# Rotations and a spread of row maxima in a hybrid attention block: one product of plain numbers against two of rounded parts

## The reference

```python
def apply_axial_rope(x, cos, sin):
    xs = x.reshape(shp[0], shp[1], shp[2], 2, 2, ROPE_HALF)
    x1 = xs[..., 0, :]
    x2 = xs[..., 1, :]
    out = jnp.stack([x1 * cc - x2 * ss, x2 * cc + x1 * ss], axis=-2)
```

```python
def _partial_rope(u, pos):
    u1 = u[..., :half]
    u2 = u[..., half:ROPE_DIM]
    r1 = u1 * cos - u2 * sin
    r2 = u2 * cos + u1 * sin
```

```python
        m_t = jnp.maximum(inter, jnp.max(logD, axis=-1))
        w_inter = jnp.exp(inter - m_t)
        s = jnp.einsum('bhld,bhsd->bhls', qc, kc) * jnp.exp(logD - m_t[..., None])
```

## Time and profile before

| what | value |
|---|---|
| median of 3 runs | 1625.29 us (1624.4 to 1625.34) |
| the profiled execution | 1620.71 us |
| its span in the profile | 1619.0 us |
| PE busy | 1539.4 us, 95% |
| PEld busy | 1229.6 us, 76% |
| DVE, ACT, POOL busy | 747.5, 639.8, 685.0 us |
| mean granted clock of PE | 0.98 of full speed |

### The profile page before, as it was taken

The page is one execution under the profiler, slowest core; times in us unless marked ns, Lnnn a source line. Parts: engine busy times, 40 slices in busy tenths (PEclk is TensorE's granted clock), DMA queues, the critical chain, the costliest instruction groups (busy, mean ns, idle before and its releaser), DMA issues.

```text
span 1619.0 us, 25305 instructions
## 1 busy us (share of the span) xinstructions
PE 1539.4 (95%) x9954; PEld 1229.6 (76%) x9954; DVE 747.5 (46%) x1723; ACT 639.8 (40%) x1337; POOL 685.0 (42%) x660
## 2 busy tenths in 40 slices
PE   5999999999898999999998899999999989999997
PEld 3787777777587888787876687878787867766875
DVE  4434554554533434444355454733432564455253
ACT  4244444444532533333344353434332344443331
POOL 2534344443532533434334444535255434444462
PEclk9999999999999999999998899999999999999998
DMA  9111111110133222323231222222131221111221
GB/s 396 43 69 53 35 45 53 53 53 27 53 105 104 79 79 79 105 79 105 79 105 52 79 85 79 79 72 85 52 104 53 98 85 53 53 53 53 99 84 52
DMA packets 22149, 128.22 MB, mean 79 GB/s; under 512 B 2448, under 2 KB 2576, under 8 KB 8080
## 3 DMA queue, kind: packets, MB, share of 16 engines
q1 hardware_dynamic: 21888, 126.35, 22.0%
q10 hardware_dynamic: 144, 0.26, 0.1%
HBM read 124.50 MB, written 2.10 MB: 78 GB/s over the span
## 4 chain that ended last, share of the span: by engine, by line
PE 83%; DVE 8%; ACT 3%; issue 3%; POOL 2%; DMA 1%; SPq 0%; POOLq 0%; DVEq 0%; ACTq 0%
PE PS L1440 16%; PE PS L1442 15%; PE PS L1441 15%; PE PS L1520 7%; PE PS L1530 6%; PE PS L1555 6%; PE PS L1435 3%; PE PS L1436 3%; PE PS L1437 3%; DVE sm L2129 1%; PE PS L1608 1%; PE PS L1600 1%; PE PS L1453 1%; POOL WL L2450 1%; DMA XC<-in_xt 1%
## 5 line engine op out<-in xcount | busy, mean ns | idle before, releaser
L2450 POOL TENSOR_TENSOR WL<-W,WH 128x512 fp32r<-128x512 f32 x304 | 400.3, 1332 | 328.8 <-ACT WH L1711 328.2
L1440 PE MATMUL PS<-HX,WH 128*128 128x512 f32 x1008 | 420.5, 417 | 11.4 <-DVE LX L2050 3.5
L1442 PE MATMUL PS<-HX,WL 128*128 128x512 f32 x1008 | 398.7, 396 | 0.0
L1441 PE MATMUL PS<-LX,WH 128*128 128x512 f32 x1008 | 398.0, 395 | 0.0
L1440 PEld LDWEIGHTS PS<-HX,WH 128*128 128x128 f32 x1008 | 193.0, 191 | 61.5 <-issue 17.4
L1442 PEld LDWEIGHTS PS<-HX,WL 128*128 128x128 f32 x1008 | 191.8, 190 | 42.6
L1441 PEld LDWEIGHTS PS<-LX,WH 128*128 128x128 f32 x1008 | 192.9, 191 | 35.9 <-issue 2.6
L1711 ACT CAST WH<-W 128x512 fp32r<-128x512 f32 x320 | 186.8, 618 | 37.4 <-PE PS L1437 21.1
L1797 ACT ACTIVATE AR<-PS,sm 128x768 f32<-128x768 f32 (+4 forms) x160 | 115.7, 723 | 163.6 <-DVE sm L2134 93.6
L2129 DVE TENSOR_REDUCE sm<-PS 128x1 f32<-128x512 f32 (+4 forms) x224 | 150.0, 670 | 54.3 <-PE PS L1520 49.7
L2517 POOL TENSOR_SCALAR AR<-AR,sm 128x768 f32<-128x768 f32 (+1 forms) x96 | 74.8, 779 | 186.4 <-DVE sm L2145 186.4
(11 more groups left out here) (285 smaller groups left out, 2529.0 us busy)
## 6 DMA issues: line engine op xcount, KB each, us to landing
W<-in_wu SPq DMA_DIRECT2D x98, 1024.0 KB, 4.8
AR<-in_wu SPq DMA_DIRECT2D x8, 1024.0 KB, 11.2
AR<-in_biasb SPq DMA_DIRECT2D x32, 256.0 KB, 2.8
XX<-in_xt SPq DMA_DIRECT2D x2, 1024.0 KB, 6.2
out<-XX SPq DMA_DIRECT2D x8, 256.0 KB, 2.2
XC<-in_xt SPq DMA_DIRECT2D x1, 1024.0 KB, 14.4
C<-in_cc SPq DMA_DIRECT2D x1, 770.5 KB, 8.6
CS<-in_cs SPq DMA_DIRECT2D x1, 512.0 KB, 12.1
```

The source lines that it names most:

```text
L1440: e.matmul(o, wh, xh, start=(k == 0), stop=False)
L1441: e.matmul(o, wh, xl, start=False, stop=False)
L1442: t = e.matmul(o, wl, xh, start=False, stop=(k == 7))
L2450: e.tensor_tensor(WL[:, d, a:z], W[:, n % 2, a:z], WH[:, d, a:z].bitcast(F32), ALU.subtract).then_inc(*s_wl_pool.by(n, q))
```

## The change

The exchanges of the queries of mixer A, those of the sparse attention's queries and keys, and the spread of the row maxima become two products each: the rounded high part of the data, then the low part, both against the same stationary matrix, rounded once. The matrices hold only 0, 1 and -1 and the selector 0 and 1, so they have no low part. The keys of mixer A keep their plain product.

Each product needs its data split, by the same helper `parts` that splits activations elsewhere: ACT copies the data with rounding (`CAST AR_parts<-AR`), then DVE (mixer A) or POOL (sparse attention) subtracts. The parts lie in pieces of the large buffer that are free at that time, so no memory is added but the 256 columns of the rounded matrices PM. In mixer A the three tasks stand behind the gate's steps k = 1, 4 and 7 in place of 2, 3 and 6. In head 0, `row_parts` stands behind `m_decay`: ACT copies the selector, waits for the finished maxima and copies them with rounding, and DVE subtracts. SP's list is the same.

```diff
@@ mixer A, planning
+        def query_parts(pair):
+            after = [(s_qsum, (pair,)), (s_qraw, (pair, 1))] + ([(s_qrot, (pair - 1,))] if pair else [])
+            parts("q", pair, 0, qT[pair % 2][:, 0:T], after, "dve")
+
...
-                yield from gate_group(pair, 0, FX, {2: lambda: query_sums(pair, FC), 3: lambda: query_turn(pair, FC), 6: lambda: query_rope(pair)})
+                yield from gate_group(pair, 0, FX, {1: lambda: (query_sums(pair, FC), query_parts(pair)), 4: lambda: query_turn(pair, FC), 7: lambda: query_rope(pair)})
...
         key_work[1]()
+        do("rotations")
         run(query_group(0, 0, vr))
...
         query_sums(0, vr)
+        query_parts(0)
         values((4,))
         query_turn(0, vr)
@@ second block, planning
                 do("m_decay")
+                do("row_parts")
...
+        def rotate_parts(key, src, by):
+            n = rotas[key] = len(rotas)
+            if key[0] == "k":
+                free_by = [(s_vsum, (3,))]
+            else:
+                free_by = [(s_nrot, (("q", n - 2),))] if n >= 2 else [(s_den, (3,))]
+            parts("r", n, 0, src, [by] + free_by, "pool")
...
+                rotate_parts(("q", m), qr[:, m, :], (s_nq, (m,)))
                 pend.append(lambda m=m: rotate(("q", m), qr[:, m, :], (s_nq, (m,)), qp[:, m, :]))
...
+            rotate_parts(("k", m), kxr[m], (s_kr, (m,)))
@@ PE
             def a_query_turn(pair):
                 free(w, ("aqr", pair))
-                w.wait_ge(*s_qraw(pair, 1))
-                e.matmul(aqps[pair, "rot"], c("p1"), qT[pair % 2][:, 0:T], start=True, stop=True).then_inc(*s_qrot.by(pair))
+                w.wait_ge(*s_pm())
+                w.wait_ge(*s_xl_dve("q", pair, 0))
+                o = aqps[pair, "rot"]
+                e.matmul(o, rot1, high("q").at(pair, 0, T), start=True, stop=False)
+                e.matmul(o, rot1, low("q").at(pair, 0, T), start=False, stop=True).then_inc(*s_qrot.by(pair))
...
             def m_exp(hd):
                 free(w, ("mE", hd))
-                w.wait_ge(*s_nM())
-                e.matmul(mps["E", hd], selv[0:4, hd, :], nM, start=True, stop=True).then_inc(*s_eb.by(hd))
+                w.wait_ge(*s_selr())
+                w.wait_ge(*s_nMl())
+                sel = selr[:, 128 * hd:128 * hd + 128]
+                e.matmul(mps["E", hd], sel, nM_h, start=True, stop=False)
+                e.matmul(mps["E", hd], sel, nM_l, start=False, stop=True).then_inc(*s_eb.by(hd))
...
-                w.wait_ge(*ev(*k))
-                e.matmul(o, c("p2"), src, start=True, stop=True).then_inc(*s_nrot.by(key))
+                n = rotas[key]
+                w.wait_ge(*s_xl_pool("r", n, 0))
+                e.matmul(o, rot2, high("r").at(n, 0, T), start=True, stop=False)
+                e.matmul(o, rot2, low("r").at(n, 0, T), start=False, stop=True).then_inc(*s_nrot.by(key))
@@ ACT
+            def rotations():
+                w.wait_ge(*s_c())
+                e.copy(PM[:, :], c("p1", 0, 256)).then_inc(*s_pm.by())
+
+            def row_parts():
+                e.copy(selr, c("sel")[0:4]).then_inc(*s_selr.by())
+                w.wait_ge(*s_nM())
+                e.copy(nM_h, nM).then_inc(*s_nMh.by())
...
             def n_cmp_in(m):
                 w.wait_ge(*s_proj("nc", m))
+                w.wait_ge(*s_nrot(("q", m + 2)))
                 e.copy(kx[m], groups["nc", m].out).then_inc(*s_kx.by(m))
@@ DVE
+            def row_parts():
+                w.wait_ge(*s_nMh())
+                e.tensor_tensor(nM_l, nM, nM_h.bitcast(F32), ALU.subtract).then_inc(*s_nMl.by())
```

More of the change, by code:

```diff
@@ L222, in build @@
         LOW = {"y": Blocks(ARp[:, 0:KC * T]), "z": Blocks(LCt[:, :])}
+        HIGH["q"] = Blocks(*[ARp[:, 17664:18176]] * 8)
+        LOW["q"] = Blocks(ARp[:, 13824:14336], *[ARp[:, 12288:12800]] * 7)
+        HIGH["r"] = Blocks(*[ARp[:, a:a + T] for a in (15872, 16384, 15872, 16384, 12288, 13312)])
+        LOW["r"] = Blocks(ARp[:, 10240:12288], ARp[:, 12800:13312], ARp[:, 13824:14336])
+        selr, nM_h, nM_l = ARp[0:4, 17920:18432], ARp[0:4, 15424:15936], ARp[0:4, 16448:16960]
         def high(phase):
@@ L2432, in vector @@
             program(e, w, dict(silu=silu, split=split, mod_tr=mod_tr, square=square, norm_rs=norm_rs, norm2_rs=norm2_rs, rbroad=rbroad,
-                               gain=gain_, scale=scale, scale_low=scale_low, parts=parts, a_key_raw=a_key_raw, a_value=a_value, a_key_sums=a_key_sums,
+                               row_parts=row_parts, gain=gain_, scale=scale, scale_low=scale_low, parts=parts, a_key_raw=a_key_raw, a_value=a_value, a_key_sums=a_key_sums,
                                a_key_norm=a_key_norm, a_key_rope=a_key_rope, a_query_raw=a_query_raw, a_query_sums=a_query_sums,
```

10 lines of the change are left out of this document (6 added, 4 removed).

## The result

The changed kernel took 1642.68 us, median of 4 runs (1639.85 to 1644.92), against 1625.28 us before; the ratio is 1.0117, 95% interval 1.0098 to 1.0136, so 1.2% slower. Timed again in experiment 12 it was 1645.89 us against 1623.47, ratio 1.0133 (1.0112 to 1.0154). The forecast was 1636.6 with a range of 1629 to 1643. The direction was right. The size was not: the recorded ratio times the median of before, 1.0117 x 1625.28, is 1644.3, 1.3 us above the range, and the second timing lies further out. (The ratio is not the plain quotient of the two medians, which is 1.0107; the first median by itself, 1642.68, stands 0.3 us inside the range.)

The account below looks back on a forecast made before the run. TensorE was taken to bound the kernel. Savings of 7.2 and 1.8 against waits of 3.5, 5.5, 5.3 and 0.7 gave +6.0 us, +11.3 with the clock: 1632.0, plus 4.6 for the median, 1636.6 us, range 1629 to 1643.

Parts of the forecast that it names:

- The products: 18 rotations and spreads on PE: two rounded products take 0.46 us instead of 0.86, saving 0.40 each, -7.2 us.
- Pair 0: Pair 0's rotation: PE waits for the parts from the copy on ACT and subtraction on DVE, +3.5 us.
- Rival (f): A rounded pair costs PE as much as the plain product, weights being loaded twice: 1643.8 us, chance 0.03.
- The query sums: Pairs 1 to 5: sums stand one gate step earlier, so PE waits 1.1 us in each, +5.5 us.
- The row maxima: Head 0: the output gate's weight copies and low parts stand behind the maxima, so PE waits, +5.3 us.
- The waits that shrink: Pair 7: -1.9 us and +0.4 from the later rotation; pair 1: -0.3; together -1.8 us.
- no wait of 1.9 in pair 7: Sign that the forecast is right: PE's wait of 1.90 us for the gate's product in pair 7 disappears.
- The sparse attention: Extra low parts on POOL make PE wait before the third rotation, less at the fourth: +0.7 us (0 to 1.5).
- the keys' rotations have several microseconds: Sparse attention: the keys' rotations have several microseconds of room, so no wait was counted for them.
- The clock: Half clock behind the long waits (2.1 and 1.6 us) and one of five waits at the sums (1.6): +5.3 us.
- rival (c): The clock falls at the sums of all five pairs: +17.7 us, 1643.0 us, chance 0.13.
- The base: The profiled execution, 1620.71 us, lies 4.6 below the median of the runs, 1625.29; that difference was added to the forecast.

Follow-up runs that it names:

- experiment 12: The changed kernel timed and profiled again with no edit: 1645.89 us, ratio 1.0133 against the kernel before.
- Experiment 7: The kernel before with only the query sums of pairs 1 to 7 moved behind gate step k = 1, nothing rounded: 1631.76 us, ratio 1.0053.
- experiment 3: The changed kernel with the row maxima's parts in head 0 moved behind the whole output gate: 1641.50 us, ratio 1.0114 against the kernel before.
- experiment 2: The changed kernel with the sparse attention's two key rotations as one plain product each, without parts: 1637.87 us, ratio 1.0096 against the kernel before.
- experiment 6: The changed kernel with the sparse attention's four query rotations as one plain product each, keys still in parts: 1640.32 us, ratio 1.0102 against the kernel before.
- experiment 8: The changed kernel with the low parts of the sparse attention's keys made on VectorE instead of GpSimd: 1640.23 us, ratio 1.0102 against the kernel before.
- experiment 4: The changed kernel with pair 0's exchange moved behind the last values and two gate steps: 1639.17 us, ratio 1.0097 against the kernel before.
- experiment 1: The changed kernel with query sums and parts of pairs 1 to 7 back behind gate step k = 2: 1637.37 us, ratio 1.0083 against the kernel before.
- experiment 5: The changed kernel with sums behind k = 2, exchange behind 6, plain keys, maxima's parts behind half the output gate, pair 0's exchange later: 1624.83 us, ratio 1.0008.
- experiment 9: The kernel of experiment 5 with the exchange of pairs 1 to 7 behind gate step k = 5 instead of 6: 1625.53 us, ratio 1.0013 to the kernel before.
- experiment 10: The kernel before with only the second block changed: query rotations and row maxima in parts as in experiment 5, keys plain: 1621.25 us, ratio 0.9987.
- experiment 11: The kernel before with only mixer A changed, as in experiment 9, second block untouched: 1626.72 us, ratio 1.0023.

## Why the prediction fell short

**The products** were right: 0.46 us per rounded pair, 0.40 saved where the pair stands among wide products, 0.31 in pairs 5 and 6, where it stands behind transposes. Rival (f) is out. Over the 18 products that is about -7.0.

**Pair 0** was right: 3.52 us against 3.5, released by DVE, with a fall of 1.7 us.

**The query sums** were right in their idle time: 0.93 to 0.96 against 1.1, five pairs. Experiment 7 shows the same in a kernel in which nothing else is changed.

**The row maxima** were too dear: 3.29 us against 5.3. The cause was right (experiment 3), and so was the thought that DVE is faster beside an idle POOL, but it was applied to two of the four operations. The two running sums and maxima, 2.22 and 2.20 us in the trace of before at 968.38 and 972.26, were left at their length, and they fell to 1.21 each: 2.0 us, the whole difference.

**The waits that shrink** were put too high, -1.8. Pair 1's wait grew from 1.24 to 1.38. In pair 7 the forecast had the wait of 1.90 vanish and nothing come in its place; 1.88 came ahead of the scores, so its sign "no wait of 1.9 in pair 7" did not come true, and 0.75 are left of the gain. Together about -0.6.

**The sparse attention** was too cheap. Its 0.7 for the queries was right: 0.30 and 0.33 us ahead of the third and fourth rotation. The step "the keys' rotations have several microseconds" looked only at the rotation itself. That has its time; PE does not wait there. What the low parts delay stands in the same queue behind them: POOL's low parts of weights, through them the buffer, the next load 4.9 us later, and at last a projection that waits 3.19. Experiments 2, 6 and 8 shorten this wait from three sides, and their profiles show the chain link by link. The waits next to it fell by 0.2, so 3.0 are left. The terms as they were measured, -7.0 + 3.5 + 4.7 + 3.3 - 0.6 + 0.6 + 3.0, make +7.5, against +6.0 forecast. That this is near is luck: the row maxima were 2.0 too dear, and the late wait and the waits that shrink, 3.0 and 1.2, were missing. The means of the executions give +7.7 (+6.5 by the first four against that same mean of before), and 1.6 more with the idle time of pair 7 put right; what is over the 7.5 is within their scatter of some 2 us.

**The clock** is the term that failed: +5.3 forecast, +13.3 measured, or 11.7 without the fall of pair 7. The mechanism was in the forecast, with 1.6 us per fall; the runs show 1.7. The count was wrong. Of the waits at the sums one of five was taken to bring a fall. Over the eight profiles that have this wait (the changed kernel twice, experiments 2, 3, 4, 6, 7 and 8) it was 25 of 40, of 1.7 us in 20 cases and of 3.4 in five, 1.3 per wait and 6.4 for five waits where 1.6 was forecast; over the six that have the sums without it (before, experiments 1, 5, 9, 10 and 11) it was 0 of 30. The falls behind the thin products of the heads spoke for this, and the forecast left them to its rival (c), which gave 1643.0. That was the better case, though its number was met by another sum: falls at three or four of the pairs, not five, and the sparse attention, which it did not have either. And the wait in the sparse attention, which the forecast did not have, stands ahead of a stretch with products of 62 and 32 columns among those of 512: in two of the five profiles with this wait of over 3 us (the changed kernel, experiment 1) the clock then stayed down for some 17 us, 8.6 us lost at once. In the other three (experiments 3, 4 and 12) it had short falls there, of 1.7 us each.

The Trainium skill (TensorE: Matmul & The Clock Gate, What's actually happening) says that the throttled state is the default and that activity releases it. The trace of the changed kernel agrees for the three pauses of 3.2 to 3.5 us, each of which is followed by a lower clock. For the release it agrees only in part: from 1312 to 1324 TensorE was busy all the time by its rows (4.00 of 4.00 us) and stayed at 0.50.

**The base** was right in kind. The profiled execution of before, 1620.71, stood below the median of the runs, and 29 runs of that kernel range from 1618.35 to 1627.0. A single profile of this program is uncertain by several microseconds, mostly through the clock, and the range should have held that too.

## What to carry to other kernels

Ask of an operation put into a queue not only who needs its result, but what stands behind it there, down to the buffer that this frees and the load that waits for the buffer. If a wait of about a microsecond can't be avoided, rather have it ahead of wide products: ahead of the narrow ones it cost 2.6 us or more in 25 cases of 40, the fall included, and ahead of the wide ones only itself. From a wait of 2 to 3.5 us wide products did not protect here. When a wait seems to have shrunk, look at the clock of the stretch before it: slower products may only have filled it. And a cheaper product is worth its saving only where its preparation is out of the way: of this change only the second block's part, with plain keys and with the parts of the row maxima behind half of the output gate, came out faster, by 0.13% (0.03 to 0.23).

## What was not expected of the hardware

A wait of 1.33 us ahead of products of 512 columns left the granted clock at 1.00 four times of four, while one of 0.95 ahead of twelve two-column products was followed by half clock 25 times of 40 (experiment 1, and eight profiles of seven kernels that share this wait). The changed kernel profiled twice, with the same instructions and idle times, had three such falls and then four (experiment 12). A fall behind these sums cost 1.7 us or 3.4. A wait of 3.3 ahead of the output gate was followed by one in six profiles and not in the seventh (experiment 1, 1.00 from 978 to 994). One of 1.88 ahead of pair 7's scores had a fall in eight profiles (the changed kernel twice, experiments 1, 2, 3, 4, 6 and 8) and none in three (5, 9 and 11). What decides is open. Four-partition operations of VectorE took 1.2 and 0.7 us beside an idle POOL, and 2.2 and 1.6 beside a busy one (experiment 3); the running sums and maxima suffer as much as the two-input subtraction does.
